# Two output projections of a transformer block as seven block products instead of eight on one Trainium2 core

## What is computed

```
def conv_branch(a, conv_w, conv_b, ln_g, ln_b, w_out):
    ...
    u = jax.nn.silu(layer_norm(u, ln_g, ln_b))
    return u @ w_out                                  # (256 x 1024) @ (1024 x 2048)

def sgu_branch(uv, ln_g, ln_b, w_s, b_s, w_out):
    ...
    return (u * v.reshape(bsz, n, SGU_DIM)) @ w_out   # (256 x 1024) @ (1024 x 2048)

def mixer_output(z, y_na, ...):
    y_conv = conv_branch(z[..., :2 * CONV_DIM], ...)
    y_sgu = sgu_branch(z[..., 2 * CONV_DIM:Q_OFF], ...)
    y_att = y_na @ w_na_out
    g_conv, g_sgu, g_att = jnp.split(jax.nn.sigmoid(z[..., G_OFF:]), N_BRANCH, axis=-1)
    return (g_conv * y_conv + g_sgu * y_sgu + g_att * y_att) @ w_o + b_o
```

## Time and profile before

| | |
|---|---|
| median of three runs | 3095.05 us (3092.33 to 3096.12) |
| span of the profiled execution, first to last instruction | 3090.4 us |
| PE busy | 3042.7 us |
| DVE busy | 1978.8 us |
| `out_conv` and `out_sgu` on PE, from 736.8 to 872.6 us | 135.8 us |
| of it DVE busy | 40.2 us |
| of it ACT busy | 28.1 us |

### The profile page before, as it was taken

How to read it: one execution, slowest core, us unless ns; L and a number is a source line. 1 busy time by engine, 2 the same in 40 slices (tenths; PEclk the granted TensorE clock), 3 DMA queues, 4 the chain that set the end, 5 groups by cost and what they waited for, 6 DMA issues and landing times.

```text
span 3090.4 us, 49849 instructions
## 1 busy us (share of the span) xinstructions
PE 3042.7 (98%) x21871; PEld 2740.0 (89%) x21883; DVE 1978.8 (64%) x2957; ACT 331.4 (11%) x643; POOL 63.4 (2%) x121
## 2 busy tenths in 40 slices
PE   6899999999999999999999999999999999999998
PEld 3588854498899999999999999999999998898998
DVE  1039974554256577766666777776667575996665
ACT  1021000023130000111110000001002102000010
POOL 0000000020000000000000000000000000000000
PEclk9999999999999999999999999999999999999999
DMA  8899876673345565755555555555444654554443
GB/s 283 298 306 305 280 246 250 243 191 124 123 137 169 173 188 172 185 174 166 191 164 164 165 164 171 170 161 180 139 137 155 200 170 131 150 148 112 120 151 112
DMA packets 580039, 561.31 MB, mean 182 GB/s; under 512 B 24270, under 2 KB 548129, under 8 KB 570350
## 3 DMA queue, kind: packets, MB, share of 16 engines
q1 hardware_dynamic: 550368, 466.65, 49.2%
q0 software_dynamic: 11552, 80.90, 7.2%
q10 hardware_dynamic: 17901, 10.57, 1.3%
HBM read 549.56 MB, written 8.51 MB: 181 GB/s over the span
## 4 chain that ended last, share of the span: by engine, by line
PE 96%; DMA 3%; DVE 0%; ACT 0%; issue 0%; SPq 0%; ACTq 0%; DVEq 0%
PE psum L484 39%; PE psum L464 28%; PE psum L763 4%; PE psum L624 2%; PE psum L562 2%; PE psum L894 2%; PE psum L884 2%; PE psum L893 2%; PE psum L887 2%; PE psum L892 2%; PE psum L882 2%; PE psum L879 2%; DMA ring<-w_mod 1%; PE psum L937 1%; PE psum L574 1%; DMA ring<-w_in 1%
## 5 line engine op out<-in xcount | busy, mean ns | idle before, releaser
L464 PE MATMUL psum<-arena,ring 128*128 128x256 f32 (+2 forms) x3712 | 875.1, 395 | 0.6 <-ACTq L1183 0.6
L464 PEld LDWEIGHTS psum<-arena,ring 128*128 128x128 f32 x3712 | 698.5, 190 | 151.5 <-issue 64.9
L484 PE MATMUL psum<-arena 128*128 128x128 f32 x6144 | 702.8, 275 | 0.3 <-DVE arena L1771 0.3
L484 PEld LDWEIGHTS psum<-arena 128*128 128x128 f32 x6144 | 694.4, 192 | 7.2 <-issue 6.2
L484 PE MATMUL psum<-arena,ring 128*128 128x128 f32 x4224 | 486.1, 275 | 0.0
L484 PEld LDWEIGHTS psum<-arena,ring 128*128 128x128 f32 x4224 | 479.1, 192 | 0.7 <-issue 0.5
L1759 DVE TENSOR_TENSOR arena<-ring 128x2048 f32<-128x2048 f32 x96 | 220.1, 2292 | 273.5 <-PE psum L484 264.8
L1898 DVE SCALAR_TENSOR_TENSOR arena<-arena,cvec 128x2048 f32<-128x2048 f32 x60 | 141.0, 2350 | 83.6 <-DMA arena<-w_mod 83.1
L1740 DVE TENSOR_TENSOR arena<-ring,arena 128x1024 f32<-128x1024 f32 (+1 forms) x168 | 167.3, 996 | 5.4
L1740 DVE TENSOR_TENSOR arena<-arena 128x512 f32<-128x512 f32 (+7 forms) x257 | 134.3, 523 | 15.8 <-DVE arena L2662 5.7
L2519 DVE TENSOR_TENSOR arena<-ring 128x1024 f32<-128x1024 f32 x64 | 78.4, 1226 | 90.2 <-PE psum L879 89.4
(11 more groups left out here) (330 smaller groups left out, 2930.9 us busy)
## 6 DMA issues: line engine op xcount, KB each, us to landing
ring<-w_ff SPq DMA_DIRECT2D x128, 1024.0 KB, 5.7
ring<-w_in SPq DMA_DIRECT2D x88, 1024.0 KB, 7.6
arena<-w_mod POOLq DMA_DIRECT2D x64, 1024.0 KB, 5.7
ring<-ab_w_in SPq DMA_DIRECT2D x56, 1024.0 KB, 5.7
ring<-cd_w_in SPq DMA_DIRECT2D x48, 1024.0 KB, 5.8
ring<-w_mod SPq DMA_DIRECT2D x32, 1024.0 KB, 7.4
ring<-w_in SPq DMA_DIRECT2D x32, 512.0 KB, 4.8
ring<-w_o SPq DMA_DIRECT2D x16, 1024.0 KB, 5.9
```

The costliest lines, as they stand in the source:

```text
L464: mm = pe.matmul(psum[:, s, m * N:(m + 1) * N], w[:, k, m * P:(m + 1) * P], x(k)[:, 0:N], start=(j == 0), stop=(j == kt - 1))
L484: return pe.matmul(o, z, w, **kw) if tokens else pe.matmul(o, w, z, **kw)
```

## The change

`out_conv` and `out_sgu` are done by `single` instead of `one_slot`. The weight sums of each slot, `TO`, lie in the first 4096 elements of `arena`, where the residual `X` was until it was stored to HBM, and where the pairs have their sums `TX`. The input sums are `SC0` and `SU0`, in places that attention biases have left, in `cvec` and in a new small tile `fourth`; `SB`, the input sums of `gate_sgu`, moves. DVE makes the sums of slot g + 1 within step g, behind `soften_max` in an even step, and combines the products of slot g behind that; `branch` is gone. ACT copies from `STAGEA` instead of from PSUM. Here "g" counts the 16 slots of both projections.

```
+        fourth = sb("fourth", [P, 4, P])
...
-        SM, SB = [at(28912 + 1024 * i, HT, P) for i in range(4)], [at(34032 + 1024 * i, HT, P) for i in range(4)]
+        SM, SB = [at(28912 + 1024 * i, HT, P) for i in range(4)], [at(o, HT, P) for o in (22528, 23552, 34032, 37104)]
+
+        TO = [at(2048 * e, 4, 4, P) for e in range(2)]
+        SC0 = [at(34032 + 512 * i, 4, P) for i in range(3)] + [
+            cvec.rearrange("p a b -> p (a b)").rearrange("p (a b) -> p a b", b=P)]
+        SU0 = [at(35568 + 512 * i, 4, P) for i in range(3)] + [fourth[:, :, :]]
         STAGEA = at(40176, 10, P)
...
             pe.wait_ge(sem("conv_ready"), n["conv_ready"].next())
-            beside("out_conv", CV, "dve", beside_gates(14))
-            pe.wait_ge(sem("sgu_ready"), n["sgu_ready"].next())
-            beside("out_sgu", ZU, "act", beside_gates(22))
+            for x, sums, base in ((CV, SC0, 14), (ZU, SU0, 22)):
+                pe.wait_ge(sem("input_sums"), n["input_sums"].next())
+                for q in range(8):
+                    single(q, halves(x, sums), TO[q % 2])
+                    beside_gates(base)(q)
...
             act.wait_ge(sem("gate_used"), n["gate_used"].next())
             for q in range(8):
-                s = q % 4
-                act.wait_ge(sem(full("act", s)), n[full("act", s)].next())
-                A(GATE[:, 2 * q:2 * q + 2, :], psum[:, s, :].rearrange("p (m t) -> p m t", m=2), ACT.Copy).then_inc(
-                    sem(free("act", s)), n[free("act", s)].up())
                 beside_gates(22)(q)
+                act.wait_ge(sem("pair_ready"), n["pair_ready"].next())
+                for m in range(2):
+                    i = 4 * (q % 2) + 2 * m
+                    ins = A(GATE[:, 2 * q + m, :].rearrange("p (a t) -> p a t", a=2), STAGEA[:, i:i + 2, :], ACT.Copy)
+                ins.then_inc(sem("stage_taken"), n["stage_taken"].up())
...
-            def branch(name, first, side):
...
-            def single_sums(name, q):
+            def single_sums(name, q, tbs=TS):
                 at_ = first_slot(name) + q
                 loaded(at_, 1)
                 w = ring[:, at_ % 4, :].rearrange("p (i f m c) -> p i f m c", f=2, m=2, c=P)
-                tb = TS[q % 2]
+                tb = tbs[q % 2]
...
             def first_taken(p):
                 if p >= 2:
                     v.wait_ge(sem("stage_taken"), p - 1)
+                if p == 7:
+                    v.wait_ge(sem("conv_ready"), 1)
+                    quarter_sums(CV, SC0, "input_sums")
+                    n["differences_used"].n = fast[0] + 8
+                    v.wait_ge(sem("differences_used"), n["differences_used"].now())
+                    single_sums("out_conv", 0, TO)
 
             gate_pairs("gate_conv", 8, -6, first_taken)
-            branch("out_conv", True, beside_gates(14))
-            for q in range(8):
-                beside_gates(22)(q)
-                if q == 4:
+            v.wait_ge(sem("gate_ready"), n["gate_ready"].next())
+            for g in range(16):
+                q, e = g % 8, g % 2
+                name, base = (("out_conv", 14), ("out_sgu", 22))[g // 8]
+                t = base + q - 4
+                if t % 2 == 0:
+                    attended(t // 2 - 1)
+                    soften_max(t // 2)
+                if g < 15:
+                    single_sums(("out_conv", "out_sgu")[(g + 1) // 8], (g + 1) % 8, TO)
+                else:
+                    w = pair_differences("gate_sgu", 0, TX)
+                if t % 2 == 0:
+                    soften(t // 2)
+                if g >= 10:
+                    v.wait_ge(sem("stage_taken"), g - 1)
+                add_products(e, 2 * e, 2 * e + 1, STAGEA)
+                o = STAGEA[:, 4 * e:4 * e + 4, :]
+                if g < 8:
+                    TT(MIX[:, 2 * q:2 * q + 2, :], o.rearrange("p (m a) t -> p m (a t)", m=2),
+                       GATE[:, 2 * q:2 * q + 2, :], ALU.mult)
+                else:
+                    v.sem_inc(sem("pair_ready"), n["pair_ready"].up())
+                if g == 5:
+                    quarter_sums(ZU, SU0, "input_sums")
+                elif g == 7:
+                    v.sem_inc(sem("gate_used"), n["gate_used"].up())
+                elif g == 13:
                     quarter_sums(HL, SB, "input_sums")
-                elif q == 6:
-                    w = pair_differences("gate_sgu", 0, TX)
+                elif g == 15:
                     pair_sums(0, w, TX)
 
             def later_taken(p):
                 if 1 <= p <= 8:
 
-                    v.wait_ge(sem("stage_taken"), 8 + p)
+                    v.wait_ge(sem("stage_taken"), 16 + p)
                     e = (p - 1) % 2
                     into_mixed(STAGEA[:, 4 * e:4 * e + 4, :], 2 * (p - 1))
+                elif p == 0:
+                    v.wait_ge(sem("stage_taken"), 15)
                 elif p >= 10:
-                    v.wait_ge(sem("stage_taken"), 8 + p - 1)
+                    v.wait_ge(sem("stage_taken"), 16 + p - 1)
                 if p == 4:
                     quarter_sums(ATT, SO, "out_sums")
                 elif p == 15:
```

## The result

The changed kernel takes 3103.29 us (median of 9 runs, 3099.93 to 3106.95), the kernel before beside it 3091.82 us (9 runs). The ratio is 1.0036, with a 95% interval of 1.0027 to 1.0044: slower, by 11.5 us. The forecast was 3102.1 us and +7.1 us. That the time lies within 1.2 us of the forecast is partly luck: the kernel before came out 3.2 us lower here than the 3095.05 us that the forecast started from, and the difference is 4.4 us larger than the sum gave; the two nearly cancel. The trace says where the 4.4 us come from: the wait came as worked out, and in some of the cycles the clock of TensorE fell as well.

A forecast was written before the change was run, and what follows sets the result against it. PE, never idle in the two projections, was taken as the bound: -11.9 us saved, +19.0 of waits, +0.1 for a late soften_max gave +7.1 us, from 3095.05 to 3102.1 us; range 3097.5 to 3107.5.

The forecast's parts named there:

- The saving of PE: In both projections, a slot's matmuls take 6.26 us instead of 7.01 and 7.00: 1.49 us less a cycle, 11.9 in eight.
- The wait: Before the second part of odd slots, PE waits for DVE's weight sums: 2.37 us a cycle, 19.0 us in eight.
- the cost of resuming: After a wait on DVE's sums, PE starts 0.06 us later and its rows take 0.11 more: 0.17 us.
- DVE's chain: From the scores' end, soften_max until 2.18 us, a 0.03 gap, 2.67 of weight sums: ready at 4.88 us.
- No second wait: In even slots, weight sums are ready 0.67 us before PE needs them; a second wait as rival had 10%.
- entry: At the stage's start, input sums and slot 0's weight sums are ready some 0.3 us before PE wants them.
- exit: At the stage's end, the first gate_sgu pair has its differences and sums made in step 15, before its second part.
- The clock: Rival: new waits lower PE's granted clock to 0.86 in all eight cycles, 20 us more, 3122 us; 3%.
- The sign: Whole kernel: chance 0.60 of slower by over 0.2%, 0.06 of faster by over 0.2%, 0.34 within.

The follow-up runs named there:

- e2: Changed kernel with odd-slot weight sums before attended and soften_max, and the products combined between soften_max and soften in even steps: 0.9974 of the kernel before, 3079.91 us.
- e6: Changed kernel with 2 extra matmuls, their result overwritten, before the weight-sum wait in each odd slot: 1.0018 of the kernel before.
- e3: Changed kernel with 8 extra matmuls, their result overwritten, before the weight-sum wait in each odd slot: 1.0022 of the kernel before.
- e7: Changed kernel with the odd slots' weight sums moved behind soften as well, so PE waits longer: 1.0148 of the kernel before.
- e8: Kernel before, with PE made to wait for the scaled probabilities after 7 of 16 matmuls in odd slots: 1.0064 of the unmodified kernel before.
- e4: Changed kernel with 4 extra matmuls, their result overwritten, before the weight-sum wait in each odd slot: 1.0024 of the kernel before.
- e5: The changed kernel itself, unmodified, measured again beside the kernel before: 1.0040 of the kernel before.

## Why the prediction was right, point by point

**The saving of PE.** Forecast 1.49 us a cycle, from `single` at 6.26 us. Where it runs without waits between attention steps (e2) the cycle is 15.66 us, so the saving is 1.31 us. The difference of 0.18 us is the change of shape: behind the scores the first part takes 2.78 us (742.01 to 744.79 in e2) instead of 2.68, and before the values the second 3.67 (767.58 to 771.24) instead of 3.58. I had taken `single` from `out_att`, where it follows itself.

**The wait.** Forecast 2.37 us with the cost of resuming. Measured 2.03 us (the first part ends at 743.98 + 2.78 = 746.76, the second starts at 748.79) and 0.09 for resuming (3.67 against 3.58), together 2.12. DVE's chain in the changed kernel is this timeline:

```profile
761.98 0.70 DVE L2059 TENSOR_TENSOR psum<-psum,arena 128x512 f32<-128x512 f32 x1 [0.73 <-PE psum L785]
762.71 1.22 DVE L2063 TENSOR_REDUCE small<-psum 128x2 f32<-128x1024 f32 x1
763.85 1.21 DVE L2089 TENSOR_TENSOR arena<-ring 128x1024 f32<-128x1024 f32 x1
765.10 0.69 DVE L1749 TENSOR_TENSOR arena<-ring,arena 128x512 f32<-128x512 f32 x1
765.83 0.69 DVE L2093 TENSOR_TENSOR arena<-ring,arena 128x512 f32<-128x512 f32 x1
```

From the scores' end (761.77) the sums are ready at 766.52, 4.75 us, forecast 4.88: the first sum starts 0.08 us before the reduction's end, where I had put a gap of 0.03. Another 0.10 us of the difference is the longer first part of the paragraph above: it takes from the saving and, as it lies within the wait, from the wait as well. So the saving was 0.18 us too large and the wait 0.25 us too large; the two errors point opposite ways, partly by that link and partly by luck. The cycle came out at +0.82 us against +0.88, and the stage without the clock at +6.55 against +7.1.

**No second wait, entry, exit.** All held: the even slots don't wait (in the first cycle their sums are ready at 755.71, 0.3 us before PE starts on them at 756.02, forecast 0.67; in the third 0.7 us before), the first slot of the stage neither, `gate_sgu` starts on time, and what follows is as long as before.

**The clock.** This is the step that was wrong. I gave it 3%, as a rival that excludes the forecast and costs 20 us in all cycles. In fact both came: the forecast's waits, and behind two or three of eight of them 1.6 us at half clock. The argument was that the opening has longer idle times at a granted clock of 1.00. It counted busy shares over 60 us and didn't ask what the clock did behind a single wait. The timeline of PE in the kernel before shows that the 1.00 can't be taken as it stands there. The same group of eight rows takes 1.94 us behind the longest wait of the opening and 1.06 us less than 5 us later; in the profile of e6, 1.94 us is what it takes in a place where the granted clock is shown as 0.50:

```profile
32.52 1.94 PE L592 MATMUL psum<-ring,cvec 128*32 128x512 f32 x8 [6.47 <-DMA ring<-w_mod]
...
37.34 1.06 PE L592 MATMUL psum<-ring,cvec 128*32 128x512 f32 x8
```

```profile
50.48 1.94 PE L600 MATMUL psum<-ring,cvec 128*32 128x512 f32 x8
```

```profile
51.00:52.00 1.00, 1.00 (x8) 0.00 (x0) 1.00 (x4) 0.00 (x0) 0.00 (x0) 0.50 0.00 0
```

All six such groups up to 34 us take 1.93 or 1.94 us, in each of the ten profiles. By their lengths PE ran at the lower level there, whatever the column says, so the opening was no evidence against the rival. And the stretch at 0.86 in the earlier trace rows is a half clock behind a wait of 1.81 us (and one of 0.41 us, a group of eight rows later, at 97.94):

```profile
96.47 1.06 PE L592 MATMUL psum<-ring,cvec 128*32 128x512 f32 x8 [1.81 <-DMA ring<-w_mod]
```

```profile
98.00:100.00 2.00, 2.00 (x5) 1.65 (x6) 0.00 (x0) 0.00 (x0) 0.00 (x0) 0.51 0.73 227
```

So the trace at hand had one wait of this length, and the clock fell behind it. The missing term is 8 waits, times a chance of about a third (known only from the runs behind: 5 of 16 in the two profiles), times 1.6 us, about 4 us more: +11.4 us as a whole and 1.0037, against 1.0036 measured. What the rival had wrong was its condition and its price: it took 0.86 for all eight cycles, and below 0.95 in the stage as the sign. The stage has 0.97 (735.55 to 882.72 us): the clock falls behind some of the waits only, and comes back each time within the 32 rows that follow.

The Trainium skill (TensorE: Matmul & The Clock Gate, What's actually happening) names idleness as what throttles the array to 1.2 GHz; e3, e7 and e8 agree, with 0, 8 and 1 half-clock cycles of eight; the stretch at 0.50 in the openings of e3 and e6, told below, came without a wait.

**The sign.** Slower by over 0.2% was given 0.60; the interval of the ratio lies wholly above. That it came out so clearly is the work of the clock: without it, as in e3, e4 and e6, the ratio is 1.0018 to 1.0024, at the edge, as forecast.

## What to carry to other kernels

A change that moves work from the bounding engine to an idle one is settled by the order on the idle one, not by its total: look in its program order for the instruction that the bound engine will wait for, and for what it stands behind. Work that depends on nothing new goes ahead of an instruction that waits, and idle time between two dependent instructions is a place for work. And when a change puts a wait of a microsecond or two in front of TensorE, price the clock behind it as well as the wait. A granted clock of 1.00 over a long stretch doesn't settle that; compare the lengths of like instructions behind single waits.

## What the runs showed of the hardware

I had not expected waits this short to matter for the clock. With a wait in each cycle of some 15 to 20 us, behind the waits of 0.97 and of 1.42 us there was no half clock in eight (one profile each), behind 1.74 us in one of eight (there at a wait of 2.10 us), behind 1.86 us in three and in two of eight (two profiles), behind 4.67 us in eight of eight. Where in the row of like waits it comes differs between executions. Each time the clock went to 1.2 GHz, 0.50 granted, and the rows behind a wait of 1.86 us took 1.6 us more, behind 4.67 us 1.4 to 2.8 us more.

Single waits do it too. Between 40 and 180 us, where PE waits for transfers, the ten profiles have 12 waits of 1.7 to 2.3 us; behind 4 of them (1.81 us in the kernel before, 1.99 and 2.19 in e5, 2.21 in e7) the clock fell to 0.50, behind the other 8, one of 2.29 us in e8 among them, it didn't. What decides between like waits isn't shown. Nor is a wait always needed: in e3 and e6 the clock fell to 0.50 at about 50.5 us with no wait longer than 0.35 us in the 10 us before, right behind 16 rows of 2 columns (L613) that PE was busy with. In the other eight profiles it stayed at 1.00 behind the same rows.
